# One normalisation on rows instead of columns, and weight conversions moved ahead of residual steps, in a two-layer transformer kernel

## The reference, cut to what matters

```
n = rmsnorm(h, g_pre_mix);  z = n @ w_in
mix = concat(short conv, rwkv7)(z) @ w_out
h = h + rmsnorm(mix, g_post_mix)                       # "w_out"
f = (silu(conv3(gate)) * up) @ w_down,  gate|up = rmsnorm(h, g_pre_ffn) @ w_gate_up
h = h + rmsnorm(f, g_post_ffn)                         # "down"
m = window attention(rmsnorm(h, norm0) @ w_in2) @ w_out2
h = h + rmsnorm(m, norm1)                              # "out2"
f = (silu(conv3(gate)) * conv3(val)) @ w_down2, gate|val = rmsnorm(h, norm2) @ w_up2
h = h + rmsnorm(f, norm3)                              # "down2"
```

## Time and profile before

| what | us |
|---|---|
| median of 3 runs | 2404.09 |
| lowest and highest | 2403.81, 2405.64 |
| the profiled execution | 2405.05 |
| its span in the profile | 2403.2 |
| PE busy | 2381.1 (99%) |
| DVE busy | 1538.9 (64%) |
| ACT busy | 1071.2 (45%) |

### The profile page before, as it was taken

One profiled execution on the slowest core, in us unless ns is written; L12 is line 12 of the kernel. 1 busy time (PEld: TensorE's weight loads), 2 busy tenths in 40 slices (PEclk: granted clock), 3 DMA queues, 4 the chain that ended last, 5 costly groups with the idle time before them and its releaser, 6 DMA issues.

```text
span 2403.2 us, 51829 instructions
## 1 busy us (share of the span) xinstructions
PE 2381.1 (99%) x20636; PEld 2233.9 (93%) x20636; DVE 1538.9 (64%) x1958; ACT 1071.2 (45%) x1365; POOL 124.4 (5%) x156
## 2 busy tenths in 40 slices
PE   9999999999999999999999999999999999999997
PEld 9999999999999999999889999889888888888897
DVE  7587665664866566665444577648787787774444
ACT  5543333245543443444444446656444444444442
POOL 2000000001200000000000110003000000000000
PEclk9999999999999999999999999999999999999999
DMA  7443222345465555555555474354655555656553
GB/s 259 154 158 120 85 90 90 109 149 178 149 193 178 183 183 181 183 184 184 188 188 185 150 246 150 122 179 155 193 178 190 194 180 190 193 180 195 183 185 127
DMA packets 116958, 406.01 MB, mean 169 GB/s; under 512 B 12848, under 2 KB 19984, under 8 KB 116560
## 3 DMA queue, kind: packets, MB, share of 16 engines
q1 hardware_dynamic: 111936, 396.07, 51.2%
q10 hardware_dynamic: 4880, 7.82, 1.0%
HBM read 401.69 MB, written 2.15 MB: 168 GB/s over the span
## 4 chain that ended last, share of the span: by engine, by line
PE 95%; DVE 3%; issue 1%; ACT 1%; POOL 0%; DMA 0%; POOLq 0%; ACTq 0%; DVEq 0%
PE ps L1706 23%; PE ps L1708 12%; PE ps L1710 11%; PE ps L1712 11%; PE ps L1711 11%; PE ps L1886 5%; PE ps L1875 3%; PE ps L1682 2%; PE ps L1683 2%; PE ps L1684 2%; PE ps L1877 2%; PE ps L1876 2%; PE ps L2098 1%; PE ps L2100 1%; PE ps L2099 1%; PE ps L1963 1%
## 5 line engine op out<-in xcount | busy, mean ns | idle before, releaser
L940 DVE TENSOR_TENSOR wl<-raw,wh 128x1024 fp32r<-128x1024 f32 x744 | 912.8, 1238 | 699.1 <-ACT wh L539 698.7
L539 ACT ACTIVATE wh<-raw 128x1024 fp32r<-128x1024 f32 x744 | 778.1, 1057 | 971.4 <-PE ps L1712 363.6
L1710 PE MATMUL ps<-xh,wh 128*128 128x256 f32 (+2 forms) x2048 | 582.5, 284 | 3.7 <-DVE wl L940 2.5
L1712 PE MATMUL ps<-xh,wl 128*128 128x256 f32 (+2 forms) x2048 | 580.4, 283 | 0.0
L1711 PE MATMUL ps<-xl,wh 128*128 128x256 f32 (+2 forms) x2048 | 580.2, 283 | 0.0
L1706 PE MATMUL ps<-x,wh 128*128 128x512 f32 x1280 | 448.2, 393 | 0.8 <-DVE wl L940 0.8
L1710 PEld LDWEIGHTS ps<-xh,wh 128*128 128x128 f32 x2048 | 387.2, 189 | 6.4 <-issue 3.3
L1711 PEld LDWEIGHTS ps<-xl,wh 128*128 128x128 f32 x2048 | 387.3, 189 | 0.2
L1712 PEld LDWEIGHTS ps<-xh,wl 128*128 128x128 f32 x2048 | 386.7, 189 | 0.0
L1706 PE MATMUL ps<-act,wh 128*128 128x512 f32 x1056 | 369.7, 393 | 0.0
L1708 PE MATMUL ps<-x,wl 128*128 128x256 f32 x1280 | 357.1, 279 | 0.0
(11 more groups left out here) (296 smaller groups left out, 3186.0 us busy)
## 6 DMA issues: line engine op xcount, KB each, us to landing
raw<-in_gate_up SPq DMA_DIRECT2D x176, 512.0 KB, 3.5
raw<-in_down SPq DMA_DIRECT2D x176, 512.0 KB, 4.2
raw<-in_up SPq DMA_DIRECT2D x176, 512.0 KB, 4.1
raw<-in_w_in SPq DMA_DIRECT2D x104, 512.0 KB, 3.6
raw<-in_in SPq DMA_DIRECT2D x48, 512.0 KB, 4.3
raw<-in_w_out SPq DMA_DIRECT2D x32, 512.0 KB, 4.2
raw<-in_out SPq DMA_DIRECT2D x32, 512.0 KB, 3.6
bias<-bias_rows ACTq DMA_DIRECT2D x1, 4096.0 KB, 25.8
```

The costliest lines, as they stand in the source:

```text
L539: act.activation(wh[:, slot], raw[:, slot], ACT.Copy).then_inc(high_ready, 1)
L940: dve.tensor_tensor(wl[:, slot], raw[:, slot], wh[:, slot].bitcast(F32), ALU.subtract).then_inc(low_ready, 1)
L1710: pe.matmul(out, w_high, hi, start=(k == 0), stop=False)
L1712: last = pe.matmul(out, w_low, hi, start=False, stop=(k == 2 * per - 1))
```

## The change

1. The norm after w_out goes by the row, as input norms do: three products of 258 moving columns in place of nine of one column, a root and a reciprocal over full rows, no turning back, and 20 spare products in a row where there were 3 and 7. DVE writes `rstd_post` itself. The other three output norms stay by the column.
2. In the openings of gate_up, in2 and up2 DVE's `lows` of step c (from c = 2) come ahead of the residual step, behind the low parts of the tiles. ACT's list is as before.
3. In the first pair of both feed-forwards chunk 23 is converted right behind chunk 22: in up2 that is ahead of the last taps and of av, in gate_up ahead of av.

```diff
             def take_root(name):
                 act.wait_ge(ss_done, SUM[name] + 1)
-                if name in OUTPUTS:
...
+                if name in COLUMNS:                      # ("down", "out2", "down2")
...
                     last = act.activation(root[:, t:t + n], ps[:, b, col:col + n], ACT.Sqrt, scale=1.0 / D, bias=eps[:, 0:1])
                 last.then_inc(root_ready, 1)
+                if name in OUTPUTS:
+                    highs(kept(name), 1, kept(name) % RING)
...
                     pair(c)
                     if first:
-                        if c >= 2:
-                            lows(first + 2 * c, 2, 2 * c % RING)
                         continue
...
-            inverse_column_of("w_out")
+            inverse_root("w_out", rstd_post)
...
                     if c == 0:
+                        row = rstd_post[:, 0:n] if n > SEQ else ps[:, 3, 0:n]
                         dve.wait_ge(gained, 3 * base // 4 + 12)
-                        residual(src, n, t0, 0, 1, ps[:, 3, 0:n])
-                        residual(src, n, t0, 1, 1, ps[:, 3, 0:n])
+                        residual(src, n, t0, 0, 1, row)
+                        residual(src, n, t0, 1, 1, row)
                         dve.wait_ge(rstd_ready, 2 * XSPLIT[name])
                     for k in (2 * c, 2 * c + 1):
                         dve.wait_ge(h_ready, base + k + 1)
                         x_low_tile(name, k, t0, gain)
+                    if c >= 2:
+                        lows(first + 2 * c, 2, 2 * c % RING)
                     if c < 7:
                         residual(src, n, t0, 2 * c + 2, 2)
...
                 def upped(p):
+                    opened = isinstance(p, int) and p == 0
                     def between(x):
-                        lows(p * 16 + (first + 21 + x), 1, 1 + x)
+                        lows(p * 16 + (first + 21 + x), 1 + (opened and x), 1 + x)
...
                 upped(0)
-                lows(first + 23, 1, 3)
                 split(0)
...
+                        squares = sq_last[:, k, 0:n] if k < 2 else sq_sum[:, 0:n]
...
+                        else:
+                            last = pe.matmul(ps[:, 0, 0:n], ones[:], squares, start=(k == 0), stop=(k == 2))
...
-                if output:
+                if name in COLUMNS:
                     spare(3, 3)
...
+                elif output:
+                    spare(1, 20)
```

More of the change, by code:

```diff
@@ L371, in x_halves @@
             return (x2[:, :, 0], x2[:, :, 1]) if name == "up2" else (xh, xl)
-        def token_parts(name):
-            return [(0, 0, P), (1, P, P)] + [(2, 2 * P, TOKENS[name] - 2 * P)] * (TOKENS[name] > 2 * P)
-        root_column, inverse_column = root[:, 0:3], root[:, 4:7]
+        COLUMNS = ("down", "out2", "down2")
+        root_column, inverse_column = root[:, 0:2], root[:, 4:6]
         XSPLIT = {"w_in": 0, "gate_up": 1, "in2": 2, "up2": 3}
@@ L558, in take_root @@
                 act.wait_ge(ss_done, SUM[name] + 1)
-                if name in OUTPUTS:
[L560 to L564, removed]
+                if name in COLUMNS:
+                    act.activation(root_column, ps[:, 0:2, 0], ACT.Sqrt, scale=1.0 / D, bias=eps[:, 0:1]).then_inc(root_ready, 1)
                     highs(kept(name), 1, kept(name) % RING)
-                    act.wait_ge(row_again, OUTPUTS.index(name) + 1)
-                    act.activation(rstd_post[:, 0:n], ps[:, 2, 0:n], ACT.Copy).then_inc(rstd_ready, 1)
+                    act.wait_ge(row_again, COLUMNS.index(name) + 1)
+                    act.activation(rstd_post[:, 0:SEQ], ps[:, 2, 0:SEQ], ACT.Copy).then_inc(rstd_ready, 1)
                     return
@@ L964, in inverse_column_of @@
                 dve.wait_ge(root_ready, SUM[name] + 1)
[L965 to L969, removed]
+                dve.reciprocal(inverse_column, root_column).then_inc(column_ready, 1)
+                dve.wait_ge(row_done, COLUMNS.index(name) + 1)
             def x_low_tile(name, k, t0, gain):
@@ L1439, in pair @@
                 def pair(c):
+                    first = FIRST[name]
                     if c == 0:
+                        row = rstd_post[:, 0:n] if n > SEQ else ps[:, 3, 0:n]
                         dve.wait_ge(gained, 3 * base // 4 + 12)
-                        residual(src, n, t0, 0, 1, ps[:, 3, 0:n])
-                        residual(src, n, t0, 1, 1, ps[:, 3, 0:n])
+                        residual(src, n, t0, 0, 1, row)
+                        residual(src, n, t0, 1, 1, row)
                         dve.wait_ge(rstd_ready, 2 * XSPLIT[name])
@@ L1450, in pair @@
                     if c == 0:
-                        lows(FIRST[name] + 3, 1, 3)
+                        lows(first + 3, 1, 3)
                 return pair
@@ L1725, in square_sum @@
                 if output:
[L1726 to L1733, removed]
+                    n, x = TOKENS[name], OUTPUTS.index(name)
+                    for k in range(3):
+                        if k < 2:
+                            pe.wait_ge(last_sq, 2 * x + k + 1)
+                        else:
+                            pe.wait_ge(sq_added, SQ0[name] + SQUARES[name])
+                        squares = sq_last[:, k, 0:n] if k < 2 else sq_sum[:, 0:n]
+                        if name in COLUMNS:
+                            for b in range(2):
+                                last = pe.matmul(ps[:, b, 0:1], squares[:, P * b:P * (b + 1)], ones[:, 0:1], start=(k == 0), stop=(k == 2))
+                        else:
+                            last = pe.matmul(ps[:, 0, 0:n], ones[:], squares, start=(k == 0), stop=(k == 2))
                 else:
@@ L1738, in square_sum @@
                 last.then_inc(ss_done, 1)
-                if output:
+                if name in COLUMNS:
                     spare(3, 3)
-                    pe.wait_ge(column_ready, OUTPUTS.index(name) + 1)
+                    pe.wait_ge(column_ready, COLUMNS.index(name) + 1)
                     for row_bank, done in ((3, row_done), (2, row_again)):
-                        for b, t, m in token_parts(name):
-                            last = pe.matmul(ps[:, row_bank, t:t + m], inverse_column[0:m, b:b + 1].broadcast_to([m, P]),
-                                             ident[0:m, 0:m], start=True, stop=True)
+                        for b in range(2):
+                            last = pe.matmul(ps[:, row_bank, P * b:P * (b + 1)], inverse_column[:, b:b + 1].broadcast_to([P, P]), ident[:],
+                                             start=True, stop=True)
                         last.then_inc(done, 1)
```

## The result

The changed kernel takes 2409.37 (median of 11 runs, 2409.0 to 2410.99), the one before 2404.18 in runs beside it: a ratio of 1.0023, 95% interval 1.0014 to 1.0031. It is slower by 5.2; forecast were 5.7 and 2409.8. The span of the profiled execution went from 2403.2 to 2409.2.

What follows compares the result with a forecast made beforehand. PE was taken to bound the kernel, holding 95% of the chain. Gate_up -0.3, in2 +2.3 and up2 +3.7 gave +5.7: execution 2410.8, median 2409.8, range 2403.0 to 2413.0.

Steps and rivals of the forecast that it cites:

- The openings: Openings of gate_up, in2, up2: DVE steps of 6.43 against PE's 5.71; sums 0.3 earlier, 2.3 later, 2.1 later.
- a quarter of late starts: Openings: one step in four was taken to start late, as in2's step 2, lasting 6.6; mean step 6.43.
- POOL: Openings: POOL's second addition runs 0.09 into DVE's low; 0.07 added per step, 6.3 to 6.37.
- The full block: Openings: by the skill's rule the later of DVE and POOL waits; low 0.09 late, 0.3 more over 14 steps.
- The norm: After w_out: clock stays at 2.4 GHz, gate_up's first product 2.5 earlier, at 602.6; 2.2 of it given back in gate_up's opening.
- The tail: End of up2's first pair: wait moves from chunk 23 to 24; part 3 alone costs 0.6, with late openings up2 loses 3.7.
- The share of the late openings: Up2's tail: DVE reaches the reciprocal 3.1 later, at 1688.1, which puts chunk 24 at 1717.3, 3.7 behind before.
- the tail takes the delay in: Rival, end of up2's first pair: chunk 24 is not held, up2 costs only 2.1, time 2408.2; chance 0.10.
- DVE keeps PE's pace: Rival, openings: something fills DVE's gaps, steps stay under 5.71, only gains remain, -3.3, time 2400.8; chance 0.12.
- the clock falls among the spares: Rival, w_out's norm: at 1.2 GHz 40 spare instructions take 9.4 instead of 4.9; 1.7 more, 2411.5; chance 0.10.
- steps of 6.6 throughout: Rival, openings: all 14 steps are late starts of 6.6, 0.16 x 14 more, time 2412; chance 0.06.

Runs made afterwards that it cites:

- part 1 alone: Only the norm after w_out by the row, everything else as in the kernel before: 2402.38, ratio 0.9995 (0.9986 to 1.0004).
- the kernel with ACT's copies first: Changed kernel, but in the openings ACT copies a step's two chunks ahead of its two tiles, not behind them: 2409.48, ratio 1.0025 to the kernel before.

## Why the prediction was right, point by point

**The openings.** Right in mechanism and place. The predicted rows are there: DVE idle twice per step, the step over PE's 5.71, PE waiting at chunks 10, 12 and 13, in in2 and up2 the waits at chunk 4 gone. The size of the step was off: it was given as 6.37 plus a quarter of late starts, 6.43, and it is 6.30 to 6.32. None of the 15 steps from step 2 on starts late. The late start of in2's step 2 was no chance of one in four: DVE idles 1.02 or 1.03 there in all four profiles with w_out's norm by the column, and 0.65 in the changed kernel and in part 1 alone. Why it goes with that norm is not shown. So 0.12 per step was added for nothing, and the late step of in2 as well: 6.6 forecast for the three openings, 5.3 measured. That is most of 5.7 against the 4.0 of the table. It also made me list chunk 8 in gate_up, where PE does not wait; in in2 it does.

**POOL.** I added 0.07 for its second addition running into the low. A pair of lows took 2.36 in the changed kernel, as with nothing beside it, so the 0.07 was wrong as well. The full block that the Trainium skill states ("SBUF — State Buffer", "Who interferes with whom") would have given 0.3 more in all; the low of the changed kernel shows neither. But the interference is real, as the kernel with ACT's copies first shows: the low starts at 620.83, POOL's second addition ends at 621.50, and the pair of lows takes 0.54 more. A full block would be 0.67, so this trace shows most of one. I had the right neighbour and took it for a small correction, when it was the next limit.

**The norm.** The 2.5 was right against the profile I read, and the clock stayed up as forecast. The step that failed is the reading of before: I took the fall of the clock in the norm for a property of the kernel. It was there in two of four profiles with that norm. Against the kernel before with its clock fallen at 507, the changed one with the same fall is 7.1 slower (2410.99 and 2403.92, one execution each); against the first profile, one without any fall is 3.5 slower (2408.54 and 2405.05, one each). The median, 5.2, lies between. So that 5.7 came near 5.2 was luck in part: two errors offset, 1.7 too much for the openings and the tail, and, if half of the executions had nothing to win in the norm, about 1.2 too little. That half is an estimate from four profiles.

**The tail.** Part 3 is right to its size: +0.6 forecast, +0.64 measured alone and +0.65 in the changed kernel, the wait moved from chunk 23 to chunk 24, DVE idle during ACT's copy of av. The share of the late openings was too large: DVE's reciprocal was to start 2.1 behind the start of up2's sum and starts 1.73 behind it, for 1.13 before. So the tail cost 1.2 and not 1.6, the wait before chunk 24 is 1.57 and not 2 to 3, and the delay shows as a wait at chunk 21 that was not forecast. The rival that the tail takes the delay in is refuted: up2's opening costs 1.65 and behind its sum 1.2 more are lost.

**The rivals.** That DVE keeps PE's pace is refuted by adds 6.32 apart. That the clock falls among the spares did not happen in any of nine profiles, and steps of 6.6 throughout did not come either.

## What to carry to other kernels

In a step that passes work between two engines and back, something independent has to lie between handing over and taking back. Of two such pieces, moving both to one side makes the step serial (6.3 for 5.5), while one on each side serves both purposes. Where an engine's step is only 0.2 shorter than that of the engine which bounds the kernel, a sum of its durations does not tell what a new order costs: the order of its waits has to be written out.

A stall behind a chain of waits moves when one link is put earlier at the cost of the next: look at the second consumer before taking the first one's gain. And before a slow stretch in one profile is priced, a second profile of the same kernel should be read.

## What the runs showed of the hardware

- The granted clock fell to 1.2 GHz in the norm by the column, whose sums move one column, although the profile counts PE as fully busy there (4.00 of 4.00). It also fell in the one profile without spares, where PE was idle for 4.58. Behind 258-column products and 40 spare instructions it did not fall in nine profiles, three of which had fallen at 507. With the norm by the column it fell in the norm in the two profiles where it had not fallen at 507, and not in the two where it had. Why one excludes the other is open.
- A DVE subtraction of 1024 columns took 1.76 beside a POOL addition and 1.22 alone; a wait that looked like pure loss had kept the two apart.
